# Gathers of expert rows for 32 tokens by four slots, in place of 64 tokens by two

## What is computed

```
q   = t @ wq                            # 8 heads, 2 halves of 128
s1, s2 = q . k1, q . k2                 # 128 keys each
sc, idx = top 16 of (top16(s1) + top16(s2))      # per token and head
gate = softmax(sc)
act[n, k] = gate[n, k] * gelu( dot(t[n], u[idx[n, k]]) )      # k = 0..127 slots
y[n]      = sum_k act[n, k] * v[idx[n, k]]
x = x + gate2 * y
```

## Time and profile before

| | us |
|---|---|
| three executions, median | 1930.86 |
| lowest, highest | 1923.73, 1937.14 |
| the profiled execution, whole | 1922.51 |
| its span | 1920.7 |
| PE busy in the span | 1527.7 |
| DVE busy | 1334.4 |
| ACT busy | 419.1 |
| POOL busy | 584.6 |

### The profile page before, as it was taken

One profiled execution on the slowest core, in us unless ns is written; L12 is line 12 of the kernel. 1 busy time (PEld: TensorE's weight loads), 2 busy tenths in 40 slices (PEclk: granted clock), 3 DMA queues, 4 the chain that ended last, 5 costly groups with the idle time before them and its releaser, 6 DMA issues.

```text
span 1920.7 us, 22276 instructions
## 1 busy us (share of the span) xinstructions
PE 1527.7 (80%) x7828; PEld 920.6 (48%) x7828; DVE 1334.4 (69%) x3962; ACT 419.1 (22%) x1139; POOL 584.6 (30%) x551
## 2 busy tenths in 40 slices
PE   7999899776757979888889687998889875655555
PEld 7644675433213757656557265765656631111111
DVE  5767656868886779675445777877844579778655
ACT  1212201000002722622211264154120210000001
POOL 0011133344442322322322322232232244454441
PEclk9999799677677999999899899999999897776877
DMA  9888589999998977987999997699699999999995
GB/s 370 338 321 321 195 353 421 421 421 419 419 421 336 421 287 259 420 329 278 401 409 410 407 407 316 234 388 369 236 393 397 413 366 421 421 422 420 422 422 221
DMA packets 100255, 703.32 MB, mean 366 GB/s; under 512 B 15264, under 2 KB 15648, under 8 KB 16560
## 3 DMA queue, kind: packets, MB, share of 16 engines
q0 software_dynamic: 78336, 570.46, 73.6%
q1 hardware_dynamic: 21808, 131.45, 16.9%
HBM read 700.82 MB, written 1.05 MB: 365 GB/s over the span
## 4 chain that ended last, share of the span: by engine, by line
PE 39%; DMA 25%; DVE 16%; issue 5%; ACT 4%; POOL 1%; DVEq 0%; POOLq 0%; ACTq 0%
PE PS L1648 15%; DMA ub<-in_peer_uv,idx 10%; DMA vb<-in_peer_uv,idx 9%; PE PS L1798 3%; PE PS L2015 3%; PE PS L1991 3%; DMA ring<-in_peer_uv,idx 3%; PE PS L1704 2%; PE PS L1972 2%; DVE vb L1149 2%; DVE ub L1149 2%; DMA mods<-in_peer_uv,idx 2%; PE PS L1875 1%; DMA ring<-in_gdn_z 1%; PE PS L1893 1%
## 5 line engine op out<-in xcount | busy, mean ns | idle before, releaser
L1648 PE MATMUL PS<-ub,z 128*64 128x512 f32 x832 | 321.4, 752 | 110.6 <-DVE z L1115 110.4
L1648 PE MATMUL PS<-vb,z 128*64 128x512 f32 x816 | 309.2, 739 | 122.1 <-DVE z L1115 114.8
L2052 POOL DMA_INDIRECT ub<-in_peer_uv,idx x208 | 232.3, 1117 | 493.1 <-PE PS L1648 424.4
L2052 POOL DMA_INDIRECT vb<-in_peer_uv,idx x204 | 218.2, 1070 | 469.4 <-PE PS L1648 419.3
L1361 ACT ACTIVATE tanhs<-cubed 128x2 f32<-128x2 f32 x256 | 52.0, 203 | 872.2 <-DVE cubed L1104 871.2
L1648 PEld LDWEIGHTS PS<-vb,z 128*64 128x64 f32 x816 | 71.5, 158 | 267.7 <-DVE z L1115 173.2
L1648 PEld LDWEIGHTS PS<-ub,z 128*64 128x64 f32 x832 | 74.4, 161 | 260.8 <-DVE z L1115 166.2
L1149 DVE CUSTOM_DVE_ANT_0 ub<-ub,h 128x1024 f32<-128x1024 f32 x104 | 127.1, 1222 | 46.6 <-DMA ub<-in_peer_uv,idx 45.7
L1149 DVE CUSTOM_DVE_ANT_0 vb<-vb,h 128x1024 f32<-128x1024 f32 x102 | 124.8, 1223 | 39.6 <-DMA vb<-in_peer_uv,idx 38.9
L1108 DVE SCALAR_TENSOR_TENSOR acts<-tanhs,gated_x 128x2 f32<-128x2 f32 x256 | 40.6, 159 | 152.6 <-ACT tanhs L1361 152.5
L1648 PE MATMUL PS<-mods,z 128*64 128x512 f32 x208 | 125.9, 736 | 23.3 <-DVE z L1115 23.0
(11 more groups left out here) (364 smaller groups left out, 2800.9 us busy)
## 6 DMA issues: line engine op xcount, KB each, us to landing
ring<-in_gdn_qkv SPq DMA_DIRECT2D x32, 1024.0 KB, 9.7
ring<-in_peer_wq SPq DMA_DIRECT2D x23, 1024.0 KB, 9.9
two_slots<-in_ada_wide POOLq DMA_DIRECT2D x20, 1024.0 KB, 6.3
ring<-in_gdn_z SPq DMA_DIRECT2D x16, 1024.0 KB, 9.8
ring<-in_gdn_w_out SPq DMA_DIRECT2D x16, 1024.0 KB, 9.4
ring<-in_gla_w_in SPq DMA_DIRECT2D x6, 2048.0 KB, 9.4
mods<-in_ada_wide POOLq DMA_DIRECT2D x11, 1024.0 KB, 6.6
ring<-in_ada_w SPq DMA_DIRECT2D x4, 2048.0 KB, 11.8
```

The costliest lines, as they stand in the source:

```text
L1648: last = pe.matmul(y[64 * g:64 * g + 64, e, :], z[:, i % 4, g, :], rows[:, D + e * 512:D + (e + 1) * 512], start=False, stop=False, skip_g ...
L2052: pool.indirect_dma_start(row_buffers[b], None, uv_rows, off).then_inc(row_landed[b].sem, 16)
```

## The change

A gather brings rows for 32 tokens by four slots. Four gathers (g = 0 to 3) form a set, with one tile `z` of four 128x32 blocks and eight products of 32 rows, four of them side by side in the columns of the array. The small operations on two columns become operations on four, once per set. h lies in four forms (`h_quarters` and `h` itself) that are all made from the transposed hT, also in stretches 0 and 1. There is one set of the lower three forms for all stretches, so that these are copied out at the end of the stretch before. The pieces of `idx` and `gate` become 16 operations of 32 partitions each. A buffer comes free when its set is done.

```diff
-            h_lower = [mods[:, 6, :], vb[:, 8, :]]
+            third = sb(scr, "third", [P, D])
+            h_quarters = [mods[:, 6, :], vb[:, 8, :], third[:]]
+            Q = P // 4
...
-            z = sb(scr, "z", [P, 4, 2, P // 2])
+            z = sb(scr, "z", [P, 4, 4, Q])
...
-                    turn.append((b, 16 * (len(users[b]) + 1), users[b][-1] // 2 + 1 if users[b] else 0))
+                    turn.append((b, 16 * (len(users[b]) + 1), users[b][-1] // 4 + 1 if users[b] else 0))
...
-                        for s in range(2):
-                            for g in range(2):
-                                here = chosen[g * 64:(g + 1) * 64]
-                                last = dve.tensor_tensor(by_half(idx, k, s, g), here[:, :, 0, s::2], here[:, :, 1, s::2], ALU.add)
+                        for s in range(4):
+                            for g in range(4):
+                                here = chosen[g * Q:(g + 1) * Q]
+                                last = dve.tensor_tensor(by_quarter(idx, k, s, g), here[:, :, 0, s::4], here[:, :, 1, s::4], ALU.add)
...
-                                if g:
+                                if g == 3:
                                     ins.then_inc(v_chain.sem, 1)
-                                    dotted = v_chain.next()
-                                    if n > 1:
-                                        spread_weight(i - 1, weighed)
-                                    gelu_argument(i, dotted)
-                                elif n:
+                                    gelu_argument(i, v_chain.next())
+                                elif g == 0 and n:
                                     weighed = weight(i - 1)
+                                elif g == 1 and n > 1:
+                                    spread_weight(i - 1, weighed)
...
+                    def quarter_out(w, g):
+                        n = QUARTERS.index(g)
+                        if w and g < 3:
+                            act.wait_ge(z_ready.sem, z_ready.at(w * STRETCH // 4))
+                        for e in range(2):
+                            act.wait_ge(h_twice.sem, h_twice.at(8 * w + 2 * n + e + 1))
+                            to = h[:, w % 2, :] if g == 3 else h_quarters[g]
+                            act.activation(to[:, e * 512:(e + 1) * 512], PS[:, banks_of(w, g)[e], :], ACT.Copy).then_inc(h_ready.sem, 1)
...
-                            for n in range(1, STRETCH, 2):
-                                i = (w * STRETCH + n) // 2
+                            for n in range(3, STRETCH, 4):
+                                i = (w * STRETCH + n) // 4
                                 yield dot_at(w, min(n + 2, STRETCH - 1)) + 0.5
...
                                 for e in range(2):
-                                    for g in range(2):
-                                        rows = row_buffers[row_turn[2 * i + g][0]]
-                                        last = pe.matmul(y[64 * g:64 * g + 64, e, :], z[:, i % 4, g, :], rows[:, D + e * 512:D + (e + 1) * 512], start=False, stop=False, skip_group_check=True)
+                                    for g in range(4):
+                                        rows = row_buffers[row_turn[4 * i + g][0]]
+                                        last = pe.matmul(y[Q * g:Q * g + Q, e, :], z[:, i % 4, g, :], rows[:, D + e * 512:D + (e + 1) * 512], start=False, stop=False, skip_group_check=True)
...
+                    def quarter(w, g):
+                        ht = hTm[:, :, Q * g:Q * g + Q] if w >= 2 else hT[:, :, w * P + Q * g:w * P + Q * g + Q]
+                        if g in (1, 2) and w == 0 or g == 1:
+                            pe.wait_ge(h_ready.sem, h_ready.at(8 * w + (2 if g == 1 else 4)))
+                        if g == 2 and w:
+                            pe.wait_ge(ffn_gate.sem, ffn_gate.at(w))
+                        for e in range(2):
+                            for j in range(4):
+                                for s in range(4):
+                                    last = pe.matmul(PS[Q * s:Q * s + Q, banks_of(w, g)[e], j * P:(j + 1) * P], ht[:, 4 * e + j, :], ident[:], start=True, stop=True)
+                            last.then_inc(h_twice.sem, 1)
...
-                        halves_by_token(0, ((2, 0), (3, 4)))
+                        for part in QUARTERS:
+                            quarter(0, part)
                         yield 1.0
-                        pe.wait_ge(h_ready.sem, h_ready.at(4))
+                        pe.wait_ge(h_ready.sem, h_ready.at(8))
...
+                            pe.wait_ge(h_ready.sem, h_ready.at(8 * t + 16))
...
-                            halves_by_channel(((2, 7), (3, 4)))
+                            for part in (3, 0, 1):
+                                quarter(2 + t, part)
+                            yield dot_at(1 + t, 125)
+                            quarter(2 + t, 2)
```

More of the change, by code:

```diff
@@ L1084, in softmax, with quarter_of @@
                         link(dve.reciprocal(total[:], total[:]))
-                        for s in range(2):
-                            for g in range(2):
-                                here = slice(g * 64, (g + 1) * 64)
-                                last = dve.tensor_tensor(by_half(gate, k, s, g), mine[here, :, s::2], total[here, :].unsqueeze(2).to_broadcast([64, 2, TOPK // 2]), ALU.mult)
+                        for s in range(4):
+                            for g in range(4):
+                                here = slice(g * Q, (g + 1) * Q)
+                                last = dve.tensor_tensor(by_quarter(gate, k, s, g), mine[here, :, s::4], total[here, :].unsqueeze(2).to_broadcast([Q, 2, TOPK // 4]), ALU.mult)
                         last.then_inc(gates_ready.sem, 1)
-                    def half_of(w, g):
-                        return h[:, w % 2, :] if g else h_lower[w % 2]
+                    def quarter_of(w, g):
+                        return h[:, w % 2, :] if g == 3 else h_quarters[g]
                     def gelu_argument(i, dotted):
-                        k, c = 2 * i // SP_, 2 * i % SP_
-                        pair = dots[:, k % 2, c:c + 2]
+                        k, c = 4 * i // SP_, 4 * i % SP_
+                        pair = dots[:, k % 2, c:c + 4]
                         dve.wait_ge(v_chain.sem, dotted)
@@ L1101, in gelu_argument @@
                         dve.wait_ge(gates_ready.sem, gates_ready.at(k + 1))
-                        dve.tensor_tensor(gated_x[:], pair, gate[:, k % IDX, c:c + 2], ALU.mult)
+                        dve.tensor_tensor(gated_x[:], pair, gate[:, k % IDX, c:c + 4], ALU.mult)
                         dve.wait_ge(v_chain.sem, made)
@@ L1420, in mixer @@
                         yield JOB_AT[NJ - 1] + 11
-                        halves_out(1, ((3, 4), (5, 6)))
                         act.wait_ge(g_loaded.sem, 16 * 6)
                         link(act.activation(alog[:], alog[:], ACT.Exp))
+                        yield dot_at(0, 100) + 1
+                        quarter_out(1, 3)
                         for t in range(T):
                             at0 = S2_AT[t]
+                            yield dot_at(t, STRETCH - 1) + 0.45
+                            for part in range(3):
+                                quarter_out(t + 1, part)
                             yield at0
@@ L1590, in mixer @@
                             yield at0 + 465
-                            halves_out(2 + t, ((2, 7), (3, 4)))
+                            quarter_out(2 + t, 3)
                         for t in range(T):
+                            if t == 0:
+                                yield dot_at(2, STRETCH - 1) + 0.45
+                                for part in range(3):
+                                    quarter_out(3, part)
                             yield W_AT[3 + t] + 2
```

73 lines of the change are left out of this document (30 added, 43 removed).

## The result

The kernel before takes 1927.36 us (median of 11 runs), the changed kernel 1943.17 us (11 runs); the ratio is 1.0076, 95% interval 1.0046 to 1.0106. The change makes this kernel slower by some 15 us (9 to 20 by the interval), where I had forecast 5.5 us less.

A forecast was written before the change was run, and what follows sets the result against it. Transfers bound stretches 0 and 3, nearly so conv 1 and projections; in the cores v products led the chain. 6.5 - 17 - 7 + 7 + 0 + 5 = -5.5 us, from 1922.5 to 1917.0; range 1885 to 1960.

The forecast's parts named there:

- rival (b): Stretches 1 and 2, nine buffers: sets hold buffers, release 6.4 us against 7.5 of rows ahead; +28 us, 1953; chance 0.18.
- Cores: -17: Four cores: -21 us from half the v products on the chain, +4 us from DVE's smaller operations.
- Conv 0: -7: Conv 0: half of line 1648's chain share, 13.7 us, is removed; half of that taken, -7 us (0 to -14).
- conv 1: +7: Conv 1: about two rows fewer in hand at a core's end, less some gain from lighter PE: +7 us together.
- Projections: 0: Projections: at most 5 us each to win, against the same 5 us lost in stock: 0.
- Start: +6.5: Start: +3.2 us from idx operations and forms, +3.3 from the later first set; +6.5 (3 to 14), none regained in stretch 0.
- Ends of stretches: +5 (0 to 12): Ends of stretches: forms for stretches 2 and 3 +1.5 us each, later first sets of stretches 1 and 2 +1 each.
- Rival (a): Cores and conv 0: PE relief shows in full, about -35 us on the sum, 1896; chance 0.34.
- Rival (c): PE products: no four side by side, a set takes 3.7 us; about +30 us on the sum, 1955; chance 0.07.
- Rival (d): PE clock: PE idles more, projection blocks run at half speed; +22 us, 1947; chance 0.05.

The follow-up runs named there:

- b_fours: Kernel before, with a row's buffer given free only when both pairs of its group of four rows are done, nothing else changed: 1974.18 us, 1.0254.
- experiment 4: The experiment with the run b_fours: late buffer release alone in the kernel before, 1974.18 us; PE's projection wait for mixer weights 5.9 us, 22.2 in the changed kernel.
- a_proj: Changed kernel with weights and z ahead of the next dot only for sets from dot 75 of each stretch on: 1907.77 us, 0.9919 to the kernel before.
- b_first: Kernel before, still with pairs, with weights and z of a pair ahead of the dot that follows it: 1920.6 us, 0.9964.
- a_first: Changed kernel with weights and z of every set ahead of the dot that follows it: 1912.52 us, 0.9940 to the kernel before.

## Why the prediction was wrong, point by point

**The step that failed** is that of conv 1, the projections and the ends of stretches: "+7", "0" and "+5" for what the sets lose in stock. I had seen the mechanism, as rival (b), "sets hold the buffers", with a chance of 0.18. In the sum it stood at 22 us (5 in each of four places, 1 at each of two ends), more than half of it set off against a lighter PE, and (b) had 28 more. The run b_fours prices it alone: 49 us by the ratio (0.0254 x 1927). Three things were wrong in it:

- "Three rows ahead are 3 x 2.49 = 7.5 us of transfers." The count began at z. Three rows were ahead there, in the lines above too (issued from 1070.62 to 1074.14), but z stands behind the second dot after the set, which itself waits for its row. When z begins, 1.15 us behind that dot's start (1075.00 to 1076.15), the transfers have run on: the dot on the last of the three begins 6.6 us later (1082.74), not 7.5.
- "PE 1.87 (twice that at half clock)": where rows are missing PE idles and its clock is down, so the dear value is the one to take at the end of the tail, 3.4 us. From z (1076.15) to the dot on the new row (1086.86) that makes 10.7 us, or 8.2 without the row's own 2.49, where I had "6.4 us, it just fits". 8.2 less 6.6 are the 1.6 us lost in this set.
- The tails stood in no window of mine, by the wrong end of stretch 1. They lost 23.0 us of the 24.8 that the stages sum to.

**Cores: -17.** Measured -18.0. It is right by luck, by two errors that cancel: the hold, which the step did not have, costs the cores 6.5 us (b_fours), so the relief is some 24 us. The share of line 1665 on the chain fell to 42.2 us, as "half" had it.

**Conv 0: -7; conv 1: +7.** Conv 0 came out at +1.1 and +2.5, conv 1 at +4.3 and +4.3, together +12.1. The hold explains +9.3 (b_fours), 4.8 of it in conv 0; against that the relief in conv 0 is some 1 us, where the sum had 7.

**Projections: 0.** Measured +8.7; the hold alone gives +8.2, by PE's waits not in the same way (experiment 4). I had set a possible gain of 5 us each against the loss, but a PE that is lighter gathers no row for which there is no buffer.

**Start: +6.5, "and stretch 0 gives none of it back".** The first product of values came at 261.52 for 254.20, +7.3 (about 262 forecast). These are PE's lines, answering to the earlier trace rows:

```profile
213.23 7.20 PE L1686 MATMUL PS<-ident,hT 128*32 128x128 f32 x256
227.65 1.94 PE L387 MATMUL PS<-ident,h 128*128 128x128 f32 x8 [7.23 <-DVE h L410]
...
261.52 1.07 PE L1665 MATMUL PS<-ub,z 128*32 128x512 f32 x8
```

A form took 1.80 us for the 2.2 taken. But the residual sum of stretch 0 began at 598.96 for 600.26: it did give it back, though the window 254 to 600 has 416 GB/s for 419. The hold of eleven buffers costs nothing (stretch 3: 327.4 for 327.1).

**Ends of stretches: +5 (0 to 12).** Measured +23.0, of which the hold is 20.0 and idx 5.9 when each is tried alone. The 12 more idx operations of each next stretch's first routing lie in the tail; I had counted them in the start and the cores.

**Rival (a)**, "PE relief in full", -35 on the sum: at equal hold sets are worth 33 to 34 us, all costs taken off. (a) without what it took off for stock (7 and 2) comes to some -42, so most of the relief was there. The kernel got (a) and (b) at once, and I had made them alternatives. The 34 is the difference of b_fours and the changed kernel, so it adds up with the 49 by construction; the 33 comes from the other pair of runs, and 49 less 33 is +16, for +15 measured.

**Rival (c)** is refuted by the set of 1.86 us. The page of the Trainium skill that I had weighed (TensorE: Matmul & The Clock Gate, Measured speedup vs the span model) gives 3.07 times for four tiles of rows and 2.38 for three of columns. The runs here have four tiles of 32 columns in a span of 1.86 us for twice the rows of a pair: no loss shows against two side by side, and the measurement decides. **Rival (d)**: the clock fell, 0.68 for 0.77 in stretch 0, 0.89 for 0.94 in the projections, but filling PE in the tails gave some 3.5 us, not clear of noise, with part of the sets still at half clock. Its share stays open.

The time lay in the range (1885 to 1960), and within 1% of before, which had 0.35.

## What to carry to other kernels

When work is batched to relieve an engine, write down how long each batch holds its buffers, from its last input's arrival to the next transfer's landing, and start the count at the instruction in whose order the release stands, not at the release. If what stands ahead of it waits for the same transfers, the hold grows with the shortage. Then look for an order that frees the buffers sooner: here a wait on the vector engine (0.27 us in the tail, more where ACT is busy) bought back 6 us of hold, and in the stages where rows were missing it turned a change that lost 0.8% into one that gains 0.8% (a_proj). Try the same order on the kernel without the batching too: by itself it gave 0.4% there (b_first).

## What the runs showed of the hardware that was not expected

- A small operation on VectorE has nearly one price at the two sizes here: 32x8 elements 0.167 us, 64x16 elements 0.171 us.
- Sixteen products in four column tiles of 32 take 1.86 us, eight in two tiles of 64 take 1.87 us.
- Gathers and the weights of projections and queries together ran at 422 GB/s for 144 us (a_first, 912 to 1056), where the kernel before had 407; so the 407 was not yet the transfers' limit. That a shortage of buffers kept it there is argued from the earlier z, not shown alone.
